# FFN up product from the third chunk on: weights stationary, both token parts in one moving operand

## What is computed

```python
D_MODEL = 1024; SEQ = 256; D_FF = 2816; DEPTH = 2
def swiglu_ffn(x, w_up, w_down):
    gate, up = jnp.split(x @ w_up, 2, axis=-1)
    return (jax.nn.silu(gate) * up) @ w_down
for l in range(DEPTH):
    x = layer_norm(ALPHA * x + 0.5 * swiglu_ffn(x, ffn1_w_up[l], ffn1_w_down[l]), ...)
    x = layer_norm(ALPHA * x + hybrid_mixer(x, ...), ...)
    x = layer_norm(ALPHA * x + 0.5 * swiglu_ffn(x, ffn2_w_up[l], ffn2_w_down[l]), ...)
```

## Time and profile before

| what | value |
|---|---|
| time, median of 3 runs | 1118.62 us (1118.34 to 1119.22) |
| span of the profiled execution | 1117.5 us |
| PE busy | 1105.8 us, 99% |
| PE weight loads busy | 917.9 us, 82% |
| DVE busy | 752.0 us, 67% |
| ACT busy | 561.1 us, 50% |
| POOL busy | 391.1 us, 35% |
| DMA | 208.95 MB, mean 187 GB/s |
| granted PE clock | 0.999, every slice of the page in the highest tenth |

### The profile page before, as it was taken

One profiled execution on the slowest core, in us unless ns is written; L12 is line 12 of the kernel. 1 busy time (PEld: TensorE's weight loads), 2 busy tenths in 40 slices (PEclk: granted clock), 3 DMA queues, 4 the chain that ended last, 5 costly groups with the idle time before them and its releaser, 6 DMA issues.

```text
span 1117.5 us, 17726 instructions
## 1 busy us (share of the span) xinstructions
PE 1105.8 (99%) x5979; PEld 917.9 (82%) x5979; DVE 752.0 (67%) x1073; ACT 561.1 (50%) x805; POOL 391.1 (35%) x560
## 2 busy tenths in 40 slices
PE   9999999999999999999999999999999999999997
PEld 7788888997788888888888888889877888888886
DVE  6657755789977865675575555467898787565544
ACT  6545433674873554543344544336748645453540
POOL 4889975107700188998500000011275000000001
PEclk9999999999999999999999999999999999999999
DMA  9776753644565577565367575536535666657541
GB/s 287 242 228 208 247 176 113 211 136 137 157 223 192 166 224 242 184 221 187 112 201 227 159 245 192 192 91 226 164 112 160 209 199 210 211 172 241 189 150 38
DMA packets 158655, 208.95 MB, mean 187 GB/s; under 512 B 12760, under 2 KB 107128, under 8 KB 158592
## 3 DMA queue, kind: packets, MB, share of 16 engines
q1 hardware_dynamic: 155232, 202.29, 56.7%
q10 hardware_dynamic: 2592, 3.67, 1.2%
q0 software_dynamic: 768, 2.17, 0.6%
HBM read 207.02 MB, written 1.06 MB: 186 GB/s over the span
## 4 chain that ended last, share of the span: by engine, by line
PE 82%; DVE 8%; ACT 3%; issue 3%; DMA 2%; SPq 1%; POOLq 0%; POOL 0%; DVEq 0%; ACTq 0%
PE ps L744 25%; PE ps L746 25%; PE ps L745 25%; DVE wlo L1246 4%; PE ps L768 2%; DMA raw<-in_ffn_w_up 1%; DVE score L1441 1%; ACT whi L430 1%; DMA raw<-in_w_in 1%; PE ps L758 1%; PE ps L986 1%; DVE gates L1413 1%; PE ps L1123 1%; PE ps L1125 1%; PE ps L1126 1%
## 5 line engine op out<-in xcount | busy, mean ns | idle before, releaser
L1246 DVE TENSOR_TENSOR wlo<-raw,whi 128x1024 fp32r<-128x1024 f32 (+1 forms) x371 | 475.7, 1298 | 188.4 <-ACT whi L430 174.2
L430 ACT CAST whi<-raw 128x1024 fp32r<-128x1024 f32 (+1 forms) x371 | 384.7, 1044 | 287.1 <-PE ps L746 225.2
L744 PE MATMUL ps<-whi,xh 128*128 128x512 f32 x976 | 384.4, 394 | 0.2 <-DVE wlo L1246 0.2
L746 PE MATMUL ps<-whi,xl 128*128 128x512 f32 x976 | 377.8, 387 | 0.0
L745 PE MATMUL ps<-wlo,xh 128*128 128x512 f32 x976 | 377.4, 387 | 0.0
L744 PEld LDWEIGHTS ps<-whi,xh 128*128 128x128 f32 x976 | 183.3, 188 | 39.0 <-issue 3.4
L746 PEld LDWEIGHTS ps<-whi,xl 128*128 128x128 f32 x976 | 183.2, 188 | 37.8
L745 PEld LDWEIGHTS ps<-wlo,xh 128*128 128x128 f32 x976 | 183.5, 188 | 34.9
L1671 POOL TENSOR_TENSOR rstd<-var_eps,cst 128x1 f32<-128x1 f32 x12 | 18.2, 1518 | 529.8 <-DVE var_eps L1295 520.7
L744 PE MATMUL ps<-whi,hh 128*128 128x512 f32 (+1 forms) x355 | 139.5, 393 | 0.0
L746 PE MATMUL ps<-whi,hl 128*128 128x512 f32 (+1 forms) x355 | 137.7, 388 | 0.0
(11 more groups left out here) (195 smaller groups left out, 1209.3 us busy)
## 6 DMA issues: line engine op xcount, KB each, us to landing
raw<-in_ffn_w_up SPq DMA_DIRECT2D x351, 256.0 KB, 4.0
raw<-in_ffn_w_down SPq DMA_DIRECT2D x176, 256.0 KB, 3.1
raw<-in_w_in SPq DMA_DIRECT2D x128, 256.0 KB, 3.4
raw<-in_w_branch SPq DMA_DIRECT2D x32, 256.0 KB, 3.3
raw<-in_w_out SPq DMA_DIRECT2D x32, 256.0 KB, 3.8
bias_g<-bias_rows ACTq DMA_DIRECT2D x16, 192.0 KB, 3.7
raw<-in_w_in SPq DMA_DIRECT2D x16, 148.0 KB, 2.3
affine<-in_ln_g SPq DMA_DIRECT2D x4, 512.0 KB, 5.6
```

Of the source, the lines that this page charges most:

```text
L430: nc.scalar.copy(whi[:, s % RING, 0:w], raw[:, s % RAW, 0:w]).then_inc(S["hi_done"], 1)
L744: nc.tensor.matmul(o, ah, bh, start=start, stop=False)
L746: return nc.tensor.matmul(o, al, bh, start=False, stop=stop)
L1246: nc.vector.tensor_tensor(wlo[:, s % RING, 0:w], raw[:, s % RAW, 0:w], f32(whi[:, s % RING, 0:w]), ALU.subtract).then_inc(S["split_done"], 1)
```

## The change

From chunk 2 on the up product is made with weights stationary: for each block k and each of four groups of 128 columns (two of the gate, two of the up half) PE runs one matmul with 128 columns of `whi` stationary and `xh` and `xl` side by side moving (512 columns, one bank: tokens' high part in the left half, low part in the right), and one with `wlo` stationary and `xh` moving (256 columns, into the left half). That is 32 matmuls of 512 and 32 of 256 columns a chunk. The result has features on the partitions, so it is not turned; but the two halves of each bank must be added. ACT copies the right halves to SBUF (gate into `silu`, up into `h`), DVE adds the left halves, ACT takes silu, DVE multiplies, ACT rounds to `hh`, DVE takes `hl`. Each chunk fills four banks; chunk c waits for `h_split` of chunk c-2, and the down product waits at its start for `h_split` of chunk 9. Chunks 0 and 1 stay as they were; the transposes of chunk 1 now stand in the middle of chunk 2. Banks of other steps are renumbered.

```diff
-    xh = sb("xh", [P, KT, SEQ], F32R)
-    xl = sb("xl", [P, KT, SEQ], F32R)
+    x_hl = sb("x_hl", [P, 2, KT, SEQ], F32R)
+    xh, xl = x_hl[:, 0], x_hl[:, 1]
...
-    ACC = [2, 6]
-    XT = [4, 6]
+    ACC = [2, 4]
+    XT = [0, 6]
+    UP_BANKS = [(0, 6), (2, 4)]
...
-        return (4 if c == 1 else 0) + t
+        return (2 if c == 1 else 0) + t
...
+    def halves(b, g):
+
+        banks = slice(UP_BANKS[b][g], UP_BANKS[b][g] + 2)
+        return ps[:, banks, 0:SEQ], ps[:, banks, SEQ:2 * SEQ]
...
+            def feature_chunk(i, f, s, c, b):
+
+                split_hi(i, s + RING)
+                split_hi(i, s + RING + 1)
+                act.wait_ge(S["pe_used"], used(s + 4) + RING * i)
+                nc.scalar.copy(silu[:, :, :], halves(b, 0)[1]).then_inc(S["gate_low"], 1)
+                act.wait_ge(S["h_split"], steps(f, c))
+                nc.scalar.copy(h[:, 0, :, :], halves(b, 1)[1]).then_inc(S["up_low"], 1)
+                act.wait_ge(S["gate_sum"], by_features(f, c) + 1)
+                nc.scalar.activation(silu[:, :, :], silu[:, :, :], ACT.Silu).then_inc(S["gate_silu"], 1)
+                split_hi(i, s + RING + 2)
+                act.wait_ge(S["up_h"], by_features(f, c) + 1)
+                nc.scalar.copy(hh[:, bass.ds(2 * c, 2), :], h[:, 0, :, :]).then_inc(S["hh_done"], 1)
+                split_hi(i, s + RING + 3)
...
+            def feature_chunk(i, f, s, c, b, first=False):
+
+                if first:
+                    pe.wait_ge(S["h_ready"], 2 * by_tokens(f, 0) + NT)
+                else:
+                    pe.wait_ge(S["h_split"], steps(f, c - 2) + 1)
+                for q in range(4):
+                    wait_split(s + q, i)
+                    for kk in range(2):
+                        k = 2 * q + kk
+                        for g in range(2):
+                            for m in range(2):
+                                bank, at = UP_BANKS[b][g] + m, kk * 512 + g * CW + m * P
+                                nc.tensor.matmul(ps[:, bank, :], w(whi, s + q, at, at + P), x_hl[:, :, k, :],
+                                                 start=k == 0, stop=False)
+                                ins = nc.tensor.matmul(ps[:, bank, 0:SEQ], w(wlo, s + q, at, at + P), xh[:, k, :],
+                                                       start=False, stop=k == KT - 1)
+                    ins.then_inc(S["pe_used"], 1)
+                    if q == 1 and first:
+                        h_transpose(f, OLD_C - 1)
...
-                    pe.wait_ge(S["h_ready"], 2 * steps(f, NC_UP - 1) + NT)
+                    pe.wait_ge(S["h_split"], steps(f, NC_UP - 1) + 1)
                     pe.wait_ge(S["ct_ready"], l + 1)
...
                 s = s0 + UP_Q
+                pe.wait_ge(S["h_split"], steps(f, NC_UP - 2) + 1)
                 for k in range(HK - RING):
-                    if k % 2 == 0:
-                        pe.wait_ge(S["h_split"], steps(f, k // 2) + 1)
                     wait_split(s + k)
...
-                    if k == 5:
-                        h_transpose(f, NC_UP - 1, (NC_UP - 1) % 2)
...
+            def feature_chunk(i, f, s, c, b):
+
+                split_lo(i, s + RING)
+                split_lo(i, s + RING + 1)
+                dve.wait_ge(S["gate_low"], by_features(f, c) + 1)
+                nc.vector.tensor_tensor(silu[:, :, :], halves(b, 0)[0], silu[:, :, :], ALU.add
+                                        ).then_inc(S["gate_sum"], 1)
+                dve.wait_ge(S["up_low"], by_features(f, c) + 1)
+                nc.vector.tensor_tensor(h[:, 0, :, :], halves(b, 1)[0], h[:, 0, :, :], ALU.add
+                                        ).then_inc(S["up_sum"], 1)
+                split_lo(i, s + RING + 2)
+                dve.wait_ge(S["up_sum"], by_features(f, c) + 1)
+                dve.wait_ge(S["gate_silu"], by_features(f, c) + 1)
+                nc.vector.scalar_tensor_tensor(out=h[:, 0, :, :], in0=silu[:, :, :], scalar=0.5, in1=h[:, 0, :, :],
+                                               op0=ALU.mult, op1=ALU.mult).then_inc(S["up_h"], 1)
+                split_lo(i, s + RING + 3)
+                dve.wait_ge(S["hh_done"], steps(f, c) + 1)
+                k = bass.ds(2 * c, 2)
+                nc.vector.tensor_tensor(hl[:, k, :], h[:, 0, :, :], f32(hh[:, k, :]), ALU.subtract
+                                        ).then_inc(S["h_split"], 1)
```

More of the change, by code:

```diff
@@ L71 @@
 LOOP_I = (NC_UP - PEEL) // 2
+OLD_C = 2
 PAIR_IN = [(2, 0, 0), (2, 0, 3)]
@@ L440, in x_hi, with h_hi, token_chunk @@
                                    ).then_inc(S["xh_done"], 1)
[L442 to L447, removed]
+            def h_hi(f, c):
+                act.wait_ge(S["ht_done"], by_tokens(f, c) + 1)
+                nc.scalar.copy(hh[:, 2 * c:2 * c + 2, :],
+                               ps[:, 4 + c, :].rearrange("p (k n) -> p k n", k=2)).then_inc(S["hh_done"], 1)
+            def token_chunk(f, s, c):
                 for t in range(NT):
[L449 to L453, removed]
+                    wait_up(act, f, s, c, t)
+                    if c > 0:
+                        act.wait_ge(S["h_ready"], 2 * by_tokens(f, c) + t - 1)
+                    nc.scalar.activation(silu[:, t, :], ps[:, 2 * c + t, 0:CW], ACT.Silu
                                          ).then_inc(S["silu_done"], 1)
@@ L456, in up_chunk @@
                         for q in range(4):
-                            split_hi(i, s + RING + q)
-                if not first:
-                    h_hi(f, c - 1, 1 - b)
+                            split_hi(0, s + RING + q)
+                if c > 0:
+                    h_hi(f, c - 1)
+            def feature_chunk(i, f, s, c, b):
[11 more added lines that the diff above has]
+                split_hi(i, s + RING + 3)
             def prepare_angles(l):
@@ L480, in ffn @@
             def ffn(f, s0, prep):
-                for c in range(PEEL):
-                    up_chunk(0, f, s0 + 4 * c, c, c % 2, first=c == 0)
+                for c in range(OLD_C):
+                    token_chunk(f, s0 + 4 * c, c)
                     if c == 1 and prep is not None:
                         prepare_angles(prep)
+                h_hi(f, OLD_C - 1)
+                for c in range(OLD_C, PEEL):
+                    feature_chunk(0, f, s0 + 4 * c, c, c % 2)
                 with act.Fori(0, LOOP_I) as i:
                     for e in range(2):
-                        up_chunk(i, f, s0 + 4 * (PEEL + e), 2 * i + PEEL + e, (PEEL + e) % 2)
+                        feature_chunk(i, f, s0 + 4 * (PEEL + e), 2 * i + PEEL + e, (PEEL + e) % 2)
                 for k in range(HK - RING):
                     splits(s0 + UP_Q + RING + k, 1)
-                    if k == 5:
-                        h_hi(f, NC_UP - 1, (NC_UP - 1) % 2)
                     if prep is not None and k in PREP:
@@ L889, in late_pass @@
                 if stage is not None:
+                    if prep is not None:
+                        pe.wait_ge(S["bt_ready"], NQ * (prep + 1))
+                        pe.wait_ge(S["k0_ready"], NQ * (prep + 1))
                     x_transpose(stage, 0)
@@ L1278, in up_chunk @@
                         for q in range(4):
-                            split_lo(i, s + RING + q)
-                if not first:
-                    h_lo(f, c - 1, 1 - b)
+                            split_lo(0, s + RING + q)
+                if c > 0:
+                    h_lo(f, c - 1)
+            def feature_chunk(i, f, s, c, b):
[17 more added lines that the diff above has]
+                                        ).then_inc(S["h_split"], 1)
             def norm(n, s_end, i, aff, between=None):
```

84 lines of the change are left out of this document (38 added, 46 removed).

## The result

The changed kernel takes 1131.2 us (1128.5 to 1132.4, four runs), the kernel before beside it 1118.6. The ratio is 1.0104 with a 95% interval of 1.0091 to 1.0116: about 1% slower, 12.6 us. The forecast was 1125.0, slower, with a range that ends at 1131.0: the direction is right, the size is twice the forecast's 6.4 us, and the median lies 0.2 us beyond the range's end. The span of the profiled execution grew from 1117.5 to 1129.3 us, 11.8.

The account below looks back on a forecast made before the run. PE, busy 99% of the span, was taken as the bound: 1117.5 - 11.3 (matmuls, transposes) + 1.5 (wait for h) + 16.2 (waits for DVE) = 1123.9, or 1125.0 us as the median of timed runs. Range: 1113.0 to 1131.0.

Parts of the forecast that it names:

- Part 1: PE's matmuls and transposes in the up product: a gain of 2.83 us per FFN, 11.3 us in four.
- rival of bare loads: Weight loads beside wide matmuls can't start ahead: a pair takes 226 + 188 ns, the time is 1204 us; chance 0.03.
- Part 2: Start of chunk 2: PE waits 1.5 us for h of chunk 1 in f = 0, nothing in the other FFNs.
- Part 3: One turn of DVE and ACT takes 9.85 us against PE's 11.05; nothing shows in f = 2 and 3.
- Part 4: GpSimd's tables in f = 0 and 1 slow DVE's splits, h and `hl`: 10.7 us of DVE delay per FFN.
- rival with the lock on splits alone: Beside GpSimd's tables only DVE's splits are slowed, not h and `hl`: 1117.6 us, about the same; chance 0.20.
- turn beside table operations: One DVE turn while GpSimd makes tables: splits, h and `hl` wait, adding 4.9 us, 14.75 us in all.
- Part 5: PE's waits for late DVE at banks and quarter 0: 8.1 us per prepared FFN, 16.2 us in two.
- E: DVE's delay per FFN from GpSimd's table work in f = 0 and 1, put at 10.7 us.
- floor at E = 0: PE's least wait at quarter 0 even without any DVE delay from tables: 2.2 us per prepared FFN.
- longest-wait rival: Every DVE operation waits out a whole table operation, E = 13: 1130.7 us; chance 0.57 together with the forecast.

Follow-up runs that it names:

- e4: The changed kernel with GpSimd's table operations replaced by two constant fills, so it computes something else: 1116.8 us, ratio 0.9984.
- e1: The changed kernel, but PE waits for a bank only until DVE has read it, no longer until `hl` is done: 1128.5 us, ratio 1.0103.
- e3_both: The changed kernel with the edits of e1 and e2 together: 1117.1 us, ratio 0.9978.
- e10: e9 with the matmuls of each k reordered, four wide ones and then four narrow ones: 1117.0 us, ratio 0.9983.
- e9: e6 with the transposes of chunk 1 after the third quarter of chunk 2 instead of after its last: 1119.3 us, ratio 1.0000.
- e2: The changed kernel, but DVE negates `c_t` before chunk 9 and not behind down tile 8: 1125.2 us, ratio 1.0062.
- e7: The kernel before, but DVE negates `c_t` behind the split of down tile 10 instead of 8: 1128.1 us, ratio 1.0076.
- e5: e3_both with the transposes of chunk 1 at the end of chunk 2 and quarters 0 and 1 one down tile later: 1130.7 us, ratio 1.0099.
- e8: The changed kernel with only `hl` put ahead of the fourth split in DVE's order: 1125.7 us, ratio 1.0057.
- e12: e3_both with e10's order of matmuls, four wide and then four narrow for each k: 1118.5 us, ratio 0.9991.
- e6: e5 with `hl` put ahead of the fourth split in DVE's order: 1123.7 us, ratio 1.0037.
- e11: e9 with each narrow matmul one group later, so it never adds to the bank just written: 1118.3 us, ratio 0.9989.

## Why the prediction was right, and where it was off

**Part 1, right in kind, mis-sized.** The new stream gives a gain in every FFN, but 9.4 us, not 11.3. The terms: a pair takes 346.7 ns, not 226.3 + 119 = 345.3 (1152 pairs x 1.4 ns = 1.6 us), and the first 16 pairs of chunk 2 take 353.4 ns (0.11 us, 0.4 in four FFNs). The transposes in mid-chunk cost 11.72 - 16 x 0.3534 - 16 x 0.3467 = 0.52 us, as good as the 0.50 of the forecast. Together 2.1, against a gap of 1.9. Distances taken from streams of one width don't add up to that of a mixed stream. The rival of bare loads is out: 188 ns loads stand beside it all, and a pair isn't 414.

**Part 2, right, a little too dear.** 0.85 us at L797 in f = 0, at 36.83, and 1.1 with the restart, not 1.5; the other 0.64 of the 1.5 in the list of waits is the stall at 29.53 of before, now at 29.67.

**Part 3, right.** In f = 2 chunk 6 ends at 614.39 + 4 x 11.093 = 658.76 (T). DVE in that turn:

```profile
659.58 0.69 DVE L1325 TENSOR_TENSOR silu<-ps,silu 128x512 f32<-128x512 f32 x1 [1.10 <-ACT silu L481]
...
666.63 0.68 DVE L1338 TENSOR_TENSOR hl<-h,hh 128x512 f32 x1
```

The gate sum ends at T + 1.5 (forecast 1.65), `hl` at T + 8.55 (forecast 8.6), and f = 2 and 3 have no wait for DVE's chain.

**Part 4, right in kind.** The product h and `hl` are slowed, the sum from PSUM is not, and e4 shows the cause: with the tables gone h, `hl` and the splits are at 0.68, 0.68 and 1.22. This is what the rule of the Trainium skill (SBUF — State Buffer, § Who interferes with whom) adds to the trace of before; the trace agrees. The rival with the lock on splits alone is refuted by the 1518 ns. The sizes were off one by one: splits took 1.42 us on average from 87 to 137 us, where the forecast's turn beside table operations has 1.9; h and `hl`, put at 1.0 more, took 0.84 and 0.54 more on average there and 1.1 more at most. By Part 5's own formula, all waits = E - 2.6, e1's 7.0 us at quarter 0 make E about 9.6, an estimate, against 10.7.

**Part 5, right on the waits.** 16.6 us against 16.2, with restarts; 14.3 as idle time alone. Its split (4.5 at the banks and 3.6 at the quarter, per FFN) was 3.75 and 3.4. e1 confirms the rule behind it: all of PE's waits together are the slip of one chain. The floor at E = 0 was 2.2, and 1.8 in e4. That nothing later gives it back is nearly so: 1.1 us came back in the mixer of layer 0.

**What was missing: the clock, 4.4 us.** The forecast priced a wait at its length and put the matmuls behind it at nothing, without giving a reason. The runs show 3.4 and 6.8 us at half clock behind the waits at quarter 0. This and Part 1's gain, 1.9 us too high, are nearly all of the 6.2 us by which the forecast was low. The longest-wait rival came near the measured time, 1130.7, but by luck: its E = 13 would have given waits of 20.8 us, and it has no clock.

So the sum as it should have been: 1117.5 - 9.4 + 1.1 + 16.6 + 4.4 - 1.1 + 0.1 = 1129.2, against a span of 1129.3.

**Is the change worth having?** Its idea gains 9.4 us on PE, and 1117.1 us (e3_both, 0.22% less than before, the interval ends at 0.9990) is the best ratio that these edits made of it, at the edge of the 0.2% that can be told from no change; e10 is level with it (1117.0 us, 0.9983). e9 and e10 took away nearly all waits of the chain, and lost most of the gain to slower rhythms.

## What to carry to other kernels

When PE saves work by handing more to DVE, follow DVE's chain to the last point where PE needs it, and price each two-SBUF-input operation beside GpSimd at its blocked duration (0.68 us became 1.2 to 1.5). Cutting one wait of a late chain mostly moves it to the next meeting point (e1 gained nothing clear of its spread, e2 half of the loss), so cut them all. Price a long PE wait above its length: behind the stands of 2.9 to 3.8 us at quarter 0 (after, e7) the low clock cost another 1.5 to 2.8 us each.

## What the runs showed of the hardware

**The clock behind waits.** In every trace, before too, the last 4 to 8 us are at half clock; they are left out here. After stands of 3.8 and 3.0 us at quarter 0 the granted clock was 0.50 for 3.4 and 6.8 us; in e7, with other matmuls, after 2.9 us twice, for 6.8 and 3.4 us. PE had been stopped, or in small matmuls, just before each. Over all traces:

| PE's stands | clock at 0.50 around their end | it stayed high |
|---|---|---|
| 2.8 to 7.0 us | 10 of 10: after 2, e1 2, e2, e5, e7 2, e8 2 | 0 |
| 1.8 to 2.4 us | 5 of 11: e2 2.0, e3 2.0, e4 1.8 twice, e12 2.0 | 6: after 1.9, 2.0 and 2.4, e3 2.0, e4 1.8, e7 1.8 |
| 1.7 us and less | 0 | all |

In e3 alone two stands of 2.0 us went both ways. So the length of the stand doesn't decide alone; what else does, and which of the two durations comes, isn't settled by these runs.

**Several rhythms of one stream.** The same alternating 512- and 256-column matmuls ran at 346.7 or at 353.4 ns a pair. After, e1, e2 and e4 were at 346.7 but for the first half of chunk 2 in most FFNs and, in after and e2, chunk 9 of f = 0 and, in after, chunks 9 and 10 of f = 1; one FFN of e3, two of e8 and, from chunk 3 on, all of e5, e6 and e9 were at 353.4. A rhythm holds until PE is held up. Within the FFNs of these runs it changes 26 times, each time at a place where one pair took 0.42 us or more: at the transposes, at a wait or at a short hold between chunks, and never inside an undisturbed stretch. Many holds leave it as it was, and which rhythm a restart brings is open: the same transposes in the middle of chunk 2 brought 346.7 in f = 1 of after and 353.4 in f = 1 of e3. It was neither the bank (e11) nor a thing that grouping cures (e10, e12: 350 to 351 ns). Streams of 512 columns alone were at 227 ns in after and e9 alike (down product of f = 2). It also fits e3's spread of 7 us from run to run, since each FFN that changes its rhythm is worth 1.9 us, but only one execution of each kernel is profiled, so this is not shown. The cause stays open.
